# Two transformer blocks on one core: gate-bias and residual loads split and moved, condition sums placed ahead of the weight splits, gate bias joined earlier

## What is computed

```python
mod = (jax.nn.silu(c) @ w_mod[l] + b_mod[l])[:, None, :]
sa, ca, ga, sm, cm, gm = jnp.split(mod, 6, axis=-1)
...
    return (g_a * y_a + g_b * y_b) @ w_o           # y_a = heads @ w_a_up, y_b = pool @ w_b_up
...
x = x + ga * mix
x = x + gm * sq_relu_mlp(modulate(x, norm_mlp_w[l], sm, cm), w_ff1[l], w_ff2[l])
```

## Time and profile before

| | before |
|---|---|
| median of 3 runs | 2387.59 us (2387.09 to 2388.12) |
| profiled execution, its own time | 2389.14 us |
| its span, mean granted PE clock | 2387.3 us, 0.993 of full |
| PE busy | 2315.0 us (97%) |
| DVE busy | 1460.6 us (61%) |
| ACT busy | 1074.1 us (45%) |
| POOL busy | 66.8 us (3%) |
| q1, the queue that SP's loads use | 456.16 MB |
| q0, the queue that POOL's loads use | 16.94 MB |

### The profile page before, as it was taken

The page is one execution under the profiler, slowest core; times in us unless marked ns, Lnnn a source line. Parts: engine busy times, 40 slices in busy tenths (PEclk is TensorE's granted clock), DMA queues, the critical chain, the costliest instruction groups (busy, mean ns, idle before and its releaser), DMA issues.

```text
span 2387.3 us, 30850 instructions
## 1 busy us (share of the span) xinstructions
PE 2315.0 (97%) x12120; PEld 1866.7 (78%) x12120; DVE 1460.6 (61%) x2171; ACT 1074.1 (45%) x1598; POOL 66.8 (3%) x90
## 2 busy tenths in 40 slices
PE   4999999999998999999999999999999999999998
PEld 1777787766776878888888888788888888888977
DVE  2344446666687776666655555674577545568875
ACT  3443234444433364444444443454555454456654
POOL 2000000111000000000000000000000000000000
PEclk9999999999999999999999999999999999999999
DMA  9756546677778756666665565555433566443233
GB/s 315 262 177 211 196 157 209 218 262 258 258 265 304 275 179 232 238 235 231 238 214 182 187 193 183 170 183 187 160 124 124 193 217 208 142 128 101 92 124 124
DMA packets 234709, 474.84 MB, mean 199 GB/s; under 512 B 7625, under 2 KB 10033, under 8 KB 233313
## 3 DMA queue, kind: packets, MB, share of 16 engines
q1 hardware_dynamic: 230736, 456.16, 56.7%
q0 software_dynamic: 3536, 16.94, 2.1%
q10 hardware_dynamic: 320, 0.13, 0.0%
HBM read 471.10 MB, written 2.10 MB: 198 GB/s over the span
## 4 chain that ended last, share of the span: by engine, by line
PE 86%; DVE 5%; DMA 5%; ACT 2%; issue 1%; SPq 0%; POOL 0%; DVEq 0%; POOLq 0%; ACTq 0%
PE acc L1753 23%; PE acc L1755 22%; PE acc L1754 22%; DMA raw<-in_w_mod 3%; PE acc L2170 2%; PE acc L2172 2%; PE acc L2173 2%; DVE wlo L1030 2%; PE acc L2214 1%; PE turn L2228 1%; PE acc L1789 1%; PE aux L2248 1%; DVE qkv L1290 1%; DMA raw<-in_w_o 1%; ACT whi L561 1%
## 5 line engine op out<-in xcount | busy, mean ns | idle before, releaser
L1030 DVE TENSOR_TENSOR wlo<-raw,whi 128x1024 fp32r<-128x1024 f32 x674 | 820.4, 1224 | 727.5 <-ACT whi L561 722.7
L561 ACT ACTIVATE whi<-raw 128x1024 fp32r<-128x1024 f32 x674 | 708.9, 1059 | 978.5 <-PE acc L1755 829.1
L1753 PE MATMUL acc<-whi,xhi 128*128 128x512 f32 x1536 | 613.2, 399 | 11.6 <-DVE wlo L1030 9.8
L1755 PE MATMUL acc<-whi,xlo 128*128 128x512 f32 x1536 | 601.8, 392 | 0.0
L1754 PE MATMUL acc<-wlo,xhi 128*128 128x512 f32 x1536 | 601.5, 392 | 0.0
L1753 PEld LDWEIGHTS acc<-whi,xhi 128*128 128x128 f32 x1536 | 290.3, 189 | 94.3 <-issue 22.9
L1755 PEld LDWEIGHTS acc<-whi,xlo 128*128 128x128 f32 x1536 | 290.1, 189 | 62.1
L1754 PEld LDWEIGHTS acc<-wlo,xhi 128*128 128x128 f32 x1536 | 290.4, 189 | 58.1 <-issue 0.5
L1753 PE MATMUL acc<-whi,hhi 128*128 128x512 f32 x512 | 201.5, 394 | 2.0 <-DVE hlo L1051 2.0
L1755 PE MATMUL acc<-whi,hlo 128*128 128x512 f32 x512 | 199.4, 390 | 0.0
L1754 PE MATMUL acc<-wlo,hhi 128*128 128x512 f32 x512 | 199.3, 389 | 0.0
(11 more groups left out here) (323 smaller groups left out, 2409.0 us busy)
## 6 DMA issues: line engine op xcount, KB each, us to landing
raw<-in_w_ff SPq DMA_DIRECT2D x128, 1024.0 KB, 5.3
raw<-in_w_mod SPq DMA_DIRECT2D x96, 1024.0 KB, 7.5
raw<-in_w_in SPq DMA_DIRECT2D x64, 1024.0 KB, 5.7
raw<-in_b_w_in SPq DMA_DIRECT2D x45, 1024.0 KB, 5.1
raw<-in_a_w_in SPq DMA_DIRECT2D x36, 1024.0 KB, 5.1
raw<-in_w_o SPq DMA_DIRECT2D x16, 1024.0 KB, 5.2
raw<-in_a_w_out SPq DMA_DIRECT2D x16, 1024.0 KB, 5.1
raw<-in_b_w_out SPq DMA_DIRECT2D x16, 1024.0 KB, 5.0
```

The lines of the kernel that those rows point to most:

```text
L561: act.activation(whi[:, k % 2, on], raw[:, n % 4, on], ACT.Copy).then_inc(hi_ready, 1)
L1030: dve.tensor_tensor(wlo[:, k % 2, on], raw[:, LOAD_OF_UNIT[k] % 4, on], whi[:, k % 2, on].bitcast(F32), ALU.subtract)\
L1753: pe.matmul(bank, hi[:, tile(kt), tok], w_hi, start=kt == k_first, stop=False, skip_group_check=True)
L1755: mm = pe.matmul(bank, lo[:, tile(kt), tok], w_hi, start=False, stop=kt == k_first + UK * k_units - 1, skip_group_check=True)
```

## The change

1. In `split_and_sum`, each half's condition tiles are summed ahead of the split of that half and not behind it.
2. The conditions of "wo" (c8 to c15) are loaded and summed one or two weight units later: with units 3, 4, 6, 7, 8, 10, 11, 12 and not 2, 3, 4, 6, 7, 8, 10, 11.
3. `ga_b` is loaded once the second column block of "up" is done, and `gm_b` and the masks once all input tiles of the MLP are built, behind the memset of `yacc`.
4. `x` is loaded in four pieces of 512 columns (512 KB each), the second to fourth when PE has finished the first 2, 6 and 10 units of "wo"; each piece has a semaphore of its own, on which only the residual sum of its block waits.
5. `add_condition(0)` and `add_condition(1)` stand at the beginning of their column blocks on DVE, ahead of the splits.

```diff
-CONDITIONS_UP, CONDITIONS_WO, ... = (1, 3, 5, 7, 9, 11, 13, 15), (1, 2, 3, 5, 6, 7, 9, 10), ...
+CONDITIONS_UP, CONDITIONS_WO, ... = (1, 3, 5, 7, 9, 11, 13, 15), (2, 3, 5, 6, 7, 9, 10, 11), ...
...
+        pool.wait_ge(acc_freed, GROUP["up"] + 4)
         pool.dma_start(ga_b, a["b_mod"][2 * D:3 * D].partition_broadcast(P)).then_inc(bias_in, 16)
-        pool.dma_start(gm_b, a["b_mod"][5 * D:6 * D].partition_broadcast(P)).then_inc(bias_in, 16)
-        pool.dma_start(tab[:, 0:672], a["c_masks"]).then_inc(masks_in, 16)
 
         pool.wait_ge(acc_freed, GROUP["wo"])
-        pool.dma_start(res3, a["x"].rearrange("(t p) n -> p t n", p=P)).then_inc(x_in, 16)
+        for n in range(4):
+            cols = slice(n * NW, (n + 1) * NW)
+            if n:
+                pool.wait_ge(units_used, 2 * (UNIT["wo"] + 4 * n - 2))
+            pool.dma_start(res3[:, :, cols], a["x"].rearrange("(t p) n -> p t n", p=P)[:, :, cols]).then_inc(x_in[n], 16)
...
         pool.memset(yacc, 0.0).then_inc(zeroed, 1)
+        pool.dma_start(gm_b, a["b_mod"][5 * D:6 * D].partition_broadcast(P)).then_inc(bias_in, 16)
+        pool.dma_start(tab[:, 0:672], a["c_masks"]).then_inc(masks_in, 16)
...
-            if b == 0:
-                dve.wait_ge(bias_in, 32)
+            if b % 4 == 0:
+                dve.wait_ge(bias_in, 16 * (b // 4 + 1))
...
             for half in range(2):
+                sum_rows(gate_sum[c // 4 % 2], COND["sums"] + c, c % 4, (2 * half, 2 * half + 1))
                 split_halves(2 * u + half, 1)
-                sum_rows(gate_sum[c // 4 % 2], COND["sums"] + c, c % 4, (2 * half, 2 * half + 1))
...
-        SUMMED_WITH = {2: 8, 3: 9, 4: 10, 6: 11, 7: 12, 8: 13, 10: 14, 11: 15}
+        SUMMED_WITH = {3: 8, 4: 9, 6: 10, 7: 11, 8: 12, 10: 13, 11: 14, 12: 15}
...
+            if n < 2:
+                add_condition(n)
             block(4 * n + 2)
...
-            add_condition(n)
+            if n > 1:
+                add_condition(n)
...
-                if n == 0:
-                    dve.wait_ge(x_in, 16)
+                dve.wait_ge(x_in[n], 16)
...
+            if t == 0:
+                dve.wait_ge(x_in[3], 16)
```

More of the change, by code:

```diff
@@ L71 @@
 CONDITIONS_AT = [n for _ in range(3) for n in FRONT_CONDITIONS] + 8 * [0] + 32 * [1]
-CONDITIONS_UP, CONDITIONS_WO, CONDITIONS_MLP = (1, 3, 5, 7, 9, 11, 13, 15), (1, 2, 3, 5, 6, 7, 9, 10), (4, 6, 11, 13)
+CONDITIONS_UP, CONDITIONS_WO, CONDITIONS_MLP = (1, 3, 5, 7, 9, 11, 13, 15), (2, 3, 5, 6, 7, 9, 10, 11), (4, 6, 11, 13)
 CONDITIONS_LOADED = {u + 2: n for u, n in enumerate(CONDITIONS_AT)}
@@ L300, in dit_kernel @@
     first_rows_done, first_rows_added = sem("first_rows_done"), sem("first_rows_added")
-    x_in, squared, res_done, norm_ready = (sem(n) for n in ("x_in", "squared", "res_done", "norm_ready"))
+    x_in = [sem(f"x_in{n}") for n in range(4)]
+    squared, res_done, norm_ready = (sem(n) for n in ("squared", "res_done", "norm_ready"))
     zeroed, q_roped, sinks_set = sem("zeroed"), sem("q_roped"), sem("sinks_set")
```

## The result

The changed kernel takes 2370.22 us (median of 4 runs, 2369.86 to 2370.61), the kernel before 2387.72 us beside it (4 runs, 2387.09 to 2388.12): a ratio of 0.9929, 95% interval 0.9918 to 0.9941. That is 17.5 us less by the medians (17.0 by the ratio, 14.1 to 19.6). The profiled execution took 2370.61 us.

The account below looks back on a forecast made before the run. PE, busy 97% of 2387.3 us, was taken as the bound. Stalls of 5.09 us in "up" and 12.64 in "wo", 17.73 together, off 2389.14 gave 2371.4; less 1.55 to the median, 2369.9, rounded to 2370; range 2366 to 2378.

Parts of the forecast that it names:

- slow halves: Half units of 12 matmuls behind up5.0, wo3.0 and the gate sum, partly at 1.2 GHz; 1.67 and 1.69 us at the first two.
- Bias and masks: In "up": moving these loads takes 6.1 to 6.8 us of DMA from ahead of the awaited units, removing 1.17 us.
- stall 1: PE's wait at up4.0 in "up", released by DVE's split: 1.17 us, claimed to go.
- Sums ahead: In "up": sums before splits free up4's slot 1.2 us sooner and give up5.0 a lead of 1.4 us.
- stall 2: PE's wait at up5.0 in "up": 2.25 us, plus 1.67 for its slow half, claimed to go.
- x in pieces, conditions later: At wo3: 1.57 million bytes fewer ahead of its load, 3.9 us, covering 3.19; c8 also behind wo2; 4.88 us gained.
- stall 3: PE's wait at wo3.0 in "wo": 3.19 us, plus 1.69 for its slow half, claimed to go.
- The join: In "wo": add_condition(0) ahead of all splits runs 25 us sooner, so PE's gate sum no longer waits; 7.76 us gained.
- stall 4: PE's gate sum behind wo3 waiting for add_condition, with the slow first half behind it: 7.76 us lost, claimed to go.
- The second: Rival in "wo": DMA becomes the bound at 364 GB/s, a 4.9 us stall returns once or twice, 2375 to 2380; chance 0.15.
- The slower case: Rival: sums starve splits, PE waits 1.53 us a unit, 24.5 us over 16 units, 2394; chance 0.03.
- late pieces: x's 512 KB pieces in "wo" might land late behind DVE; over 9 us late needed before one counts, sum unchanged.

## Why the prediction was right, and where its parts were not

**The sum.** Forecast 17.73 us and 2370.0; measured 17.5 us and 2370.2. The four stalls and their slow halves were the whole of it, in each phase too (5.09 and 12.64 forecast, 5.29 and 12.70 in the profiles). This total needs only that all four go, not that each goes by the part named for it; that the five parts together sufficed, where the working had two of them wrong in size and one without effect, was in part luck. The first MLP matmul, "about 825", is at 824.75; the load of wo3, under 9 us, takes 7.47; up5.0's split, forecast to be done at 666.8, is done at 666.1 and PE wants it at 667.69, a lead of 1.6 for the 1.4 worked out. up2.0's lead is 0.9 for 0.6. DMA asked for 364 GB/s in "wo" by the working, and ran at 337.

**Bias and masks (1.17 us, stall 1).** Right in place: undone, 1.3 us of waits come back, 1.9 us of "up". But the working had up4's load land some 7 us sooner, 6 of them by the bias bytes, and counted from c1's issue it landed 3.7 us sooner (657.24 - 643.56 for 661.46 - 644.09). And the rest was laid on the sums alone in "up". Without the moved loads the sums leave 0.85 and 0.48, and the moved loads alone take 3.5 us out of "up", the sums alone 3.4: each removes most of what the other would.

**Sums ahead (3.92 us, stall 2).** The step that was mis-sized. It is worth 9.1 us alone and 12 when undone (8.3 and 10.5 by the profiles). The working carried the slot's earlier release forward by "1.2 us" for one unit in "up". It put the rest of up4's earlier landing down to the bias bytes. In fact the sums alone bring up6's and up7's loads 2.9 us forward, the moved loads 2.4, both together 6.3, and the lead stays through "wo": with the sums behind, ACT's waits for the weights are 80 us and not 32, and "wo" is 8.7 us longer. Nothing of that was priced in "wo".

**x in pieces, conditions later (4.88 us, stall 3).** The step "that alone covers the 3.19" holds where nothing else is changed: both loads moved alone do take the wait at wo3.0 away. But PE's time isn't won by it, since the gate sum then waits 8.2 us, and in the changed kernel the pieces give nothing. With the sums first, wo3.0 waits 0.23 us only, with x whole and the conditions in their old places. The conditions' later places guard wo8, not wo3.

**The join (7.76 us, stall 4).** The mechanism is right, the wait goes when the join stands first, but the size is not: it gave 2.6 us alone and 5.0 on top of the sums (5.0 and 6.8 by the profiles). Done alone it let PE run on into weights that were not there (wo8, 2.31 us). And the whole stall wasn't DVE's order: with all other parts in place and the join late, 1.27 us of wait are left of 4.91.

**The rivals.** None came true. The second, a wait on splits between wo7 and wo13, was the nearest: it appears as soon as the sums are behind (wo8 and wo12), or the conditions early (wo8), or the join alone is moved (wo8). It was held off by the sums, which the prediction didn't count there, so the argument made against it ("at 360 only 0.6 us is missing") was not what kept it away. The slower case didn't start: the smallest lead in "up" is 0.9 us, and sums that run while DVE waits for ACT cost no split. Nothing is seen of late pieces either: four pieces of 512 KB landed 4.8 to 7.3 us after their issue with DVE busy 86 to 88% of the time. The Trainium skill, "SBUF — State Buffer", section "SBUF: two separate sides", ties such a delay to DVE operations in its two-port modes; no run here shows in which mode DVE's sums and splits ran, so this case doesn't test that warning.

## What to carry to other kernels

Look for the loop in which a buffer comes back (here sum, slot, load, rounding, split), and put the work that frees a buffer into the time in which its engine waits anyway; here the lead so won lasted through the rest of both phases. The stalls and their slow halves give the total gain well, but which part of a change brings which microsecond isn't read from where a stall stands: parts done alone gave 9.1, 2.6 and 3.3 us, in two of three cases with a new or larger wait behind the one removed, so each part is worth a run alone and a run undone. And when two profiles are compared, count from a common event and not from the span's start: these executions reach "up" up to 3.4 us apart (634.93 to 638.31 for the same eight matmuls in two kernels that are equal up to there).

## What the runs showed of the hardware

A wait of the same size is not always followed by a slow half. In the changed kernel's first profile the wait of 1.82 us ahead of the MLP is, and the granted clock from 815 to 840 us is 0.93; in its second the wait of 1.80 at the same place isn't, and the clock is 1.00:

```profile
815.00:840.00 25.00, 23.18 (x108) 18.48 (x108) 16.30 (x27) 18.51 (x37) 2.01 (x2) 0.93 0.35 116
```

```profile
815.00:840.00 25.00, 22.78 (x111) 18.04 (x110) 17.52 (x28) 20.02 (x39) 2.02 (x2) 1.00 0.36 118
```

The spans are 2368.8 and 2367.3 us. Waits of 2.57 us (776.55, the conditions early) and 2.31 us (788.47, the join first) had none behind them either, waits of 2.23 and 2.75 us in the same stretch (the sums behind) had. Which it will be is not told by the length of the wait in these runs, so a slow half of some 1.5 us is an uncertainty of each stall that is predicted. Not all of it need reach the end: from the last matmul of "wo" to the first of the MLP's second matrix it is 53.60 us in the first profile and 52.77 in the second, 0.8 us apart.
